# A hybrid decoder block on eight cores: the convolution's rows copied on chip, and the second tile's norm moved ahead

## The reference

```
x = x + 0.5 * swiglu(rmsnorm(x, ffn1_norm), ...)           # first feed-forward
h = rmsnorm(x, mix_norm); proj = h @ w_in                  # 1024 -> 6656
glu_a, glu_b, q, k, v, g_conv, g_attn = split(proj)
u = glu_a * sigmoid(glu_b)
u = causal_depthwise_conv(u, dw_w) + dw_b                  # width 31, along the tokens
conv_out = silu(layernorm(u)) @ w_proj
attn_out = sliding_window_gqa_sinks(rope(q), rope(k), v) @ w_o
x = x + (sigmoid(g_conv) * conv_out + sigmoid(g_attn) * attn_out) @ w_out
x = x + 0.5 * swiglu(rmsnorm(x, ffn2_norm), ...)           # second feed-forward
out = rmsnorm(x, final_norm)
```

## Time and profile before

| | us |
|---|---|
| three runs | 1957.9, 1786.0, 1765.6 (median 1786.0) |
| profiled execution | 1768.8 |
| its span on the slowest core (core 5) | 1767.8 |
| spans of the eight cores | 1748.8 to 1767.8 |
| PE busy | 1638.3 (93%) |

### The profile page before, as it was taken

How to read it: one execution, slowest core, us unless ns; L and a number is a source line. 1 busy time by engine, 2 the same in 40 slices (tenths; PEclk the granted TensorE clock), 3 DMA queues, 4 the chain that set the end, 5 groups by cost and what they waited for, 6 DMA issues and landing times.

```text
span 1767.8 us, 29593 instructions; the slowest of 8 cores (1748.8 to 1767.8 us)
## 1 busy us (share of the span) xinstructions
PE 1638.3 (93%) x9060; PEld 739.0 (42%) x9060; DVE 704.0 (40%) x1180; ACT 651.8 (37%) x1396; POOL 687.7 (39%) x723
## 2 busy tenths in 40 slices
PE   6999677899988899989999999999998999998996
PEld 2555333344433334434443344444443444443442
DVE  3432422764243365441225266542224356524212
ACT  3212312664132366443222257553222258422221
POOL 1014023865332595413331387423322277413232
PEclk9999788999999999999999999999999999999998
DMA  8998987579999999985556978764443953443542
GB/s 171 197 217 167 208 204 178 140 190 183 203 196 239 233 180 172 192 274 156 163 147 176 238 198 190 194 240 152 142 138 115 237 199 98 145 152 128 182 123 81
DMA packets 118121, 315.39 MB, mean 178 GB/s; under 512 B 14544, under 2 KB 36304, under 8 KB 117968
## 3 DMA queue, kind: packets, MB, share of 16 engines
q1 hardware_dynamic: 92480, 231.46, 41.8%
q0 software_dynamic: 24768, 80.95, 29.0%
q10 hardware_dynamic: 720, 1.09, 0.2%
HBM read 327.01 MB, written 67.37 MB: 223 GB/s over the span
## 4 chain that ended last, share of the span: by engine, by line
PE 80%; DMA 11%; issue 2%; ACT 2%; DVE 2%; SPq 2%; POOL 1%; ACTq 0%; DVEq 0%; POOLq 0%
PE ps L508 74%; PE ps L82 5%; DMA RR<-ush 3%; DMA ush<-S 3%; DMA ush<-uT 2%; SPq L98 2%; DMA X<-xT 1%; DMA wt<-wall 1%; PE ps L706 1%; DMA outT<-tf 1%; ACT ps L82 0%; POOL acc L82 0%; DVE xnF L82 0%; DVE S L82 0%; ACT S L82 0%
## 5 line engine op out<-in xcount | busy, mean ns | idle before, releaser
L508 PE MATMUL ps<-xnF,wt 128*128 128x512 bf16 x2816 | 652.1, 386 | 15.9 <-DVE xnF L82 6.5
L508 PEld LDWEIGHTS ps<-xnF,wt 128*128 128x128 bf16 x2816 | 270.0, 99 | 357.2 <-issue 64.3
L508 PE MATMUL ps<-Hh,wt 128*128 128x512 bf16 x1408 | 328.6, 380 | 0.0
L508 PE MATMUL ps<-xnM,wt 128*128 128x512 bf16 x1344 | 310.9, 383 | 0.4 <-DVE xnM L82 0.2
L82 ACT ACTIVATE tf<-ps 128x512 f32<-128x512 f32 x304 | 179.9, 595 | 312.5 <-PE ps L508 291.0
L82 POOL TENSOR_TENSOR Hh<-tf 128x512 bf16<-128x512 f32 x128 | 164.7, 1287 | 187.9 <-PE ps L508 115.1
L82 DVE SCALAR_TENSOR_TENSOR tf<-tf,ps 128x512 f32<-128x512 f32 x176 | 120.4, 684 | 260.8 <-PE ps L508 248.0
L508 PEld LDWEIGHTS ps<-Hh,wt 128*128 128x128 bf16 x1408 | 134.3, 98 | 160.8 <-issue 9.3
L508 PEld LDWEIGHTS ps<-xnM,wt 128*128 128x128 bf16 x1344 | 129.9, 98 | 169.7 <-issue 22.2
L98 POOL DMA_DIRECT2D wt<-wall x121 | 67.7, 563 | 245.6 <-PE ps L508 214.5
L82 DVE SCALAR_TENSOR_TENSOR X<-ps,X 128x512 f32<-128x512 f32 x96 | 66.3, 691 | 199.5 <-PE ps L508 197.5
(11 more groups left out here) (97 smaller groups left out, 1471.8 us busy)
## 6 DMA issues: line engine op xcount, KB each, us to landing
wt<-wac SPq DMA_DIRECT2D x207, 512.0 KB, 4.8
wt<-wall POOLq DMA_DIRECT2D x121, 512.0 KB, 9.7
wac<-wt SPq DMA_DIRECT2D x82, 512.0 KB, 8.7
wt<-wdc SPq DMA_DIRECT2D x80, 352.0 KB, 3.1
RR<-ush SPq DMA_DIRECT2D x128, 135.0 KB, 6.3
wt<-wd POOLq DMA_DIRECT2D x48, 352.0 KB, 7.1
wdc<-wt SPq DMA_DIRECT2D x32, 352.0 KB, 5.8
X<-xT SPq DMA_DIRECT2D x28, 256.0 KB, 10.8
```

The costliest lines, as they stand in the source:

```text
L508: op(PE, lambda: mm(out, lhsT=pick(use.slot), rhs=rhs, start=start, stop=stop), rd, wr, t, use)
```

## The change

- `ush` is gone. `uT` gets 32 more columns: column 31 on holds the tile's 512, columns 0 to 30 the 31 tokens ahead of it. For tile 0 these 31 are computed from the halo (31 columns in place of 128); for the others they are copied by DVE from `past`, where the tile before left them (two small copies a chunk).
- `u_in` copies from `uT` to `RR` within SBUF: 16 DMAs of 32 x 540 (one for each shift k and group g) in place of 4 of 32 x 4 x 540, all on SP.
- Tile 1's squares are summed on POOL into `accL` and its norm is written to `xnF` behind the first gate/up, that is during the first down projection. The load of `X[1]` has the same condition as before (`H_b[8]`).
- The halo's squares wait for tile 0's norm (`xnF_b[7]`).
- The planner's durations of a few small tasks are set by size, and a group of 8 or more DMAs is planned at 0.35 us each.

```diff
     def dma(self, q, dsem, moves, rd=(), wr=(), t=5.0):
...
-        k.t = 0.1 * len(moves)
+        k.t = (0.1 if len(moves) < 8 else 0.35) * len(moves)
...
-        uT = sb("uT", [128, 3, NT], BF16); uT_b = bufs(3)
+        uT = sb("uT", [128, 3, 32 + NT], BF16); uT_b = bufs(3)
+        past = sb("past", [128, 8, 32], BF16); past_b = bufs(8)
...
-            f_a_norm(t, banks.get())
+            if t != 1:
+                f_a_norm(t, banks.get())
             if t == 0:
                 bk = banks.get()
-                sums_pe(Xh, Xh_b, bk, HALO)
+                sums_pe(Xh, Xh_b, bk, HALO, (xnF_b[7],))
...
             ffn_gu(0, banks, t == 0)
             keep = G.key
+            if t == 0:
+                load_x(1, (H_b[8],))
+                for c in range(8):
+                    sq_acc(accL, c == 0, X[1][:, c, :], X_b[1][c], tm=tmM)
+                normed(rstd(accL, banks.get()), C_FFN1, X[1], X_b[1], xnF, xnF_b)
...
-            parts = [(xnM, xnM_b, NT, uT[:, cc % 3, :], uT_b[cc % 3], base, ush_s[cc % 3], ush_b[cc])]
+            u_t, u_b = uT[:, cc % 3, :], uT_b[cc % 3]
+            parts = [(xnM, xnM_b, 0, NT, u_t[:, 31:31 + NT])]
             if halo:
-                parts.append((xnh, xnh_b, HALO, uh[:, cc % 2, :], uh_b[cc % 2], 0, ushh_s[cc % 2], ushh_b[cc]))
+                parts.append((xnh, xnh_b, HALO - 31, 31, u_t[:, 0:31]))
+            else:
+                COPY(u_t[:, 0:31], past[:, cc, 0:31], (past_b[cc],), (u_b,), 0.15)
...
-                dma(SP, sem, [(ush_d[cc][:, c0:c0 + N], u_t)], rd=(u_b,), wr=(db,), t=6.0)
+            COPY(past[:, cc, 0:31], u_t[:, NT:NT + 31], (u_b,), (past_b[cc],), 0.15)
 
         def u_in(cc, base):
-            dma(SP, RR_s[cc % NRR], [(RR[cc % NRR][32 * k:32 * k + 32, :, :],
-                                      ush_d[cc][:, base - 31 + k:base - 31 + k + RW].rearrange("(g c) t -> c g t", g=4)) for k in range(4)],
-                rd=(ush_b[cc], ushh_b[cc]), wr=(RR_b[cc % NRR],), t=8.0)
+            dma(SP, RR_s[cc % NRR], [(RR[cc % NRR][32 * k:32 * k + 32, g, :], uT[32 * g:32 * g + 32, cc % 3, k:k + RW])
+                                     for k in range(4) for g in range(4)], rd=(uT_b[cc % 3],), wr=(RR_b[cc % NRR],), t=6.0)
```

More of the change, by code:

```diff
@@ L363, in build_nc @@
     wdc_d = dt("wdc", [32, 128, 11 * 128], BF16, kind="Internal").ap()
-    ush_d = dt("ush", [8, 128, TL], BF16, kind="Internal").ap()
     with ExitStack() as es:
@@ L399, in build_nc @@
         RR_s = [mksem(f"s_rr{i}") for i in range(NRR)]
-        ush_b = bufs(8); ush_s = [mksem(f"s_ush{i}") for i in range(3)]
         NW = 9
@@ L435, in build_nc @@
         s_pos = [mksem(f"s_pos{i}") for i in range(2)]
-        ushh_b = bufs(8); ushh_s = [mksem(f"s_ushh{i}") for i in range(2)]
-        uh = S[:].rearrange("p a b -> p (a b)")[:, 768:896].bitcast(BF16).rearrange("p (a b) -> p a b", a=2); uh_b = bufs(2)
         s_out = [mksem(f"s_out{i}") for i in range(8)]
@@ L480, in build_nc @@
         alias(cvo_b, Xh_b + Hhh_b + [accH[1]])
-        alias(S_b, xnh_b + uh_b + [cosh_b, sinh_b])
+        alias(S_b, xnh_b + [cosh_b, sinh_b])
         def ACTF(out, in_, func, rd, wr, t=None, **kw):
@@ L514, in load_x, with proj @@
                     rd=after, wr=(X_b[t % 2][c],), t=7.0)
-        def proj(pst, pb, use, sub, rhs_t, rhs_bufs, N):
+        def proj(pst, pb, use, sub, rhs_t, rhs_bufs, N, c0=0):
             G.join(True)
             for kc in range(8):
-                MMW(pst[:, 0:N], use, lambda s, kc=kc: s[:, kc, sub * 128:(sub + 1) * 128], rhs_t[:, kc, 0:N], kc == 0, kc == 7,
+                MMW(pst[:, 0:N], use, lambda s, kc=kc: s[:, kc, sub * 128:(sub + 1) * 128], rhs_t[:, kc, c0:c0 + N], kc == 0, kc == 7,
                     rhs_bufs[kc] if isinstance(rhs_bufs[kc], list) else [rhs_bufs[kc]], (pb,), t=N / 2360)
@@ L543, in rstd, with sums_pe @@
             return pst, pb
-        def sums_pe(x_t, x_bufs, bank, N):
+        def sums_pe(x_t, x_bufs, bank, N, after=()):
             pst, pb = bank
@@ L548, in sums_pe @@
                 s_t, s_b = sqF.get()
-                ACTF(s_t[:, 0:N], x_t[:, c, 0:N], AF.Square, (x_bufs[c],), (s_b,))
-                MM(pst[:, 0:N], ones[:], s_t[:, 0:N], c == 0, c == 7, (ones_b, s_b), (pb,))
+                ACTF(s_t[:, 0:N], x_t[:, c, 0:N], AF.Square, (x_bufs[c],) + after, (s_b,), t=0.2 + 0.42 * N / NT)
+                MM(pst[:, 0:N], ones[:], s_t[:, 0:N], c == 0, c == 7, (ones_b, s_b), (pb,), t=N / 2360)
         def normed(inv, gcol, x_t, x_bufs, out_t, out_bufs, N=NT):
@@ L725, in glu @@
             use = SA.use(("A", 28 + cc), "M")
-            parts = [(xnM, xnM_b, NT, uT[:, cc % 3, :], uT_b[cc % 3], base, ush_s[cc % 3], ush_b[cc])]
+            u_t, u_b = uT[:, cc % 3, :], uT_b[cc % 3]
+            parts = [(xnM, xnM_b, 0, NT, u_t[:, 31:31 + NT])]
             if halo:
-                parts.append((xnh, xnh_b, HALO, uh[:, cc % 2, :], uh_b[cc % 2], 0, ushh_s[cc % 2], ushh_b[cc]))
-            for xn_t, xn_bufs, N, u_t, u_b, c0, sem, db in parts:
+                parts.append((xnh, xnh_b, HALO - 31, 31, u_t[:, 0:31]))
+            else:
+                COPY(u_t[:, 0:31], past[:, cc, 0:31], (past_b[cc],), (u_b,), 0.15)
+            for xn_t, xn_bufs, c0, N, dst in parts:
                 pa, pab = bM5.get()
                 pb_, pbb = bM5.get()
-                proj(pb_, pbb, use, 1, xn_t, xn_bufs, N)
+                proj(pb_, pbb, use, 1, xn_t, xn_bufs, N, c0)
                 t_t, t_b = tmM.get()
-                ACTF(t_t[:, 0:N], pb_[:, 0:N], AF.Tanh, (pbb,), (t_b,), scale=0.5)
-                proj(pa, pab, use, 0, xn_t, xn_bufs, N)
-                STT(u_t, t_t[:, 0:N], 1.0, pa[:, 0:N], ALU.add, ALU.mult, (t_b, pab), (u_b,))
-                dma(SP, sem, [(ush_d[cc][:, c0:c0 + N], u_t)], rd=(u_b,), wr=(db,), t=6.0)
+                ACTF(t_t[:, 0:N], pb_[:, 0:N], AF.Tanh, (pbb,), (t_b,), t=0.2 + 0.4 * N / 512, scale=0.5)
+                proj(pa, pab, use, 0, xn_t, xn_bufs, N, c0)
+                STT(dst, t_t[:, 0:N], 1.0, pa[:, 0:N], ALU.add, ALU.mult, (t_b, pab), (u_b,), t=0.15 + 0.55 * N / 512)
+            COPY(past[:, cc, 0:31], u_t[:, NT:NT + 31], (u_b,), (past_b[cc],), 0.15)
         def u_in(cc, base):
-            dma(SP, RR_s[cc % NRR], [(RR[cc % NRR][32 * k:32 * k + 32, :, :],
-                                      ush_d[cc][:, base - 31 + k:base - 31 + k + RW].rearrange("(g c) t -> c g t", g=4)) for k in range(4)],
-                rd=(ush_b[cc], ushh_b[cc]), wr=(RR_b[cc % NRR],), t=8.0)
+            dma(SP, RR_s[cc % NRR], [(RR[cc % NRR][32 * k:32 * k + 32, g, :], uT[32 * g:32 * g + 32, cc % 3, k:k + RW])
+                                     for k in range(4) for g in range(4)], rd=(uT_b[cc % 3],), wr=(RR_b[cc % NRR],), t=6.0)
         taps = [None]
@@ L942, in build_nc @@
         load_pos(HALO, NT, cos_t, cos_b, (H_b[4],))
-        load_x(1, (H_b[8],))
         cdma(POOL, "ident", ident[:], ident_d, ident_b, (H_b[11],))
```

## The result

The change makes the kernel slower: a median of 1909.0 us (1872.2 to 2115.0, five runs) against 1772.6 (1765.6 to 1957.9, five runs), a ratio of **1.0569, 95% interval 1.0494 to 1.0644**. The highest times on both sides come from executions in which one die or both ran at a lower clock; the ratio leaves them out, and so isn't that of the two medians. The profiled execution took 1874.9 us, 106 more than the profiled one of before. The forecast was 1747, its range ended at 1790.

The account below looks back on a forecast made before the run. PE was taken as nearly full except in the convolution stages, mostly tile 0's, where SP's waits held it up. Gains of 23 + 8 - 4 - 7 + 2 = 22 us from 1768.8 gave 1747 us, range 1706 to 1790.

Parts of the forecast that it names:

- the price of an issue: SP's row copies: 0.40 us per DMA issue, 16 making 6.4 and, with another issue, 6.9 us a chunk.
- the break-even: All convolution stages: the change becomes a loss from 7.6 us of SP a chunk, an issue of 0.44.
- the bound of 0.99 under load: SP's row copies: upper bound on one issue, from eight issues under load that took 7.92 us.
- the rival at 0.60 an issue: SP as new bound, slower than before: 10.1 us a chunk, 1849 us; chance 0.19, half near 1782, half beyond 1804.
- tile 0 with the junction: Tile 0's convolution stage: gain 14.4 us, with the junction's 12.5 less 3.6 making 23.
- The junction: Behind the first down projection: 56 gate/up matmuls of tile 1 fill PE's half-idle 17 us, gain 12.5.
- DVE's wait: DVE's copy into uT, waiting for rows to leave the buffer: counted as nothing at 6.9 us a chunk.
- The weights in tile 0: Tile 0's convolution stage: SP's waits for weights were taken to stay at 24.0 us.
- Cheap issues: Rival: issues at 0.35 us and under, PE sets the pace, 1714 us (1700 to 1733); chance 0.27.
- Weight stream binds: Rival in tile 0: stage cannot become shorter than about 100 us, gain 14 becomes 5, 1756 us; chance 0.13.
- No overlap: Rival: small transfers don't overlap, 38 us a chunk, kernel over 2500 us; chance 0.01.
- The rule on small transfers: Row copies of 34.6 KB: many transfers under 64 KB should be coalesced, so the change would go the wrong way.

## Why the prediction was wrong

**The step that failed** is the price of an issue: "I take 0.40, between the unloaded rows and nearer to them than to the loaded one. 16 x 0.40 = 6.4, and one or so other issue per chunk [...] makes 6.9 us of SP per chunk". It measured 0.591 for the issue, 0.63 to 0.76 from start to start, and 11.9, 12.0, 11.7 and 11.4 us a chunk in tiles 0 to 3. The mechanism was as forecast: SP paces the convolutions. The size of this term was off, and with it the sign of the whole, since the break-even that the prediction named lay at 7.6 us a chunk.

The price was read from reads of device memory, the only RR rows that the trace had, and corrected downwards for fewer pieces. Both moves were wrong: between 32 and 128 pieces there is no difference (0.422 against 0.429 us from device memory, 0.591 against 0.588 from SBUF), while having the source in SBUF as well as the destination, which wasn't considered, adds 0.16 to 0.17 us. The prediction did name the bound of 0.99 under load and priced the rival at 0.60 an issue, 10.1 us a chunk, with 1849 us. That rival is what happened, with a chance of 0.19, half of it beyond 1804. Its 1849 is near the measured 1875, but partly because errors cancel. Its price per us of chunk, (1849 - 1782) / (10.1 - 8.0) = 32, carried to the 11.7 us that a chunk took on the mean makes 1849 + 51 = 1900. Against that stand landings of 2.4 us in place of 6 in four stages (14 less) and the 24.0 us of weight waits that it kept in tile 0 and that weren't there; the first u of tile 0, on the other hand, came 8.6 us later than it had it (see below). That gives about 1871, an estimate from these rows. The planner's wrong duration, worth about 1.5%, stood in no term of the sum.

By its terms, forecast and measured: tile 0 with the junction +23, in fact -10.2 at the last convolution; tile 1 +8, in fact -26.9; tile 2 -4, in fact -34.2; tile 3 -7, in fact -36.4.

**The junction** was right: full, at a clock of 1.00. Alone the move brings about 15 us (ratio 0.9918) where 12.5 less 3.6 stood in the sum. One step beside it was missed: 12.5 us of matmuls in 7.9 us of idle time also push the first u back, so "u of chunk 0 is there at 190.2" became 198.8 (197.80, plus 0.98 for its two parts). In the change the gain couldn't come out in tile 0, where SP set the end of the stage; it came back behind it, as the 9.4 us of the ledger.

**DVE's wait**: "so I count nothing; at 10 us a chunk it would be late". It was, for 170.7 us, and the condition was the right one. A fourth buffer took 29 us of it away and changed no time.

**The weights in tile 0**: the waits for them were taken as fixed at 24.0 us. In the profile after, SP's waits from 186 to 310 us hold none for `wt<-wall`: its issues fill the time in which it used to wait. So tile 0's stage, which was 100 us long already, grew by 1.9 us from its first u and not by 27 to 36, as the others did. "SP's waits for weights stay at 24.0" was a second step that failed, in the change's favour.

**The rivals.** Cheap issues: refuted by 0.591. Weight stream binds ("the stage cannot become shorter than about 100"): in the kernel with four on-chip DMAs the last convolution of tile 0 starts at 252.26, 55 us after the first u at 197.11; refuted. No overlap: refuted, 2.4 us landings behind issues of 0.6. **The rule on small transfers**, quoted in the prediction from the Trainium skill, "DMA: Bandwidth & Descriptors", "Rules for kernel authors", pointed the right way. What was paid by each, though, was SP's issue and not the transfer, which landed faster than the large ones (2.4 us against 6.3).

## What to carry to other kernels

Before a change multiplies the number of DMAs, count the issuing queue's time for one unit of work and set it against the time of the engine it feeds; and take the price of an issue from a row whose source and destination lie where yours do. When such a queue is full, share the work with an idle engine until neither is late, since moving all of it only moves the bound: 8 DMAs and 8 DVE copies a chunk gave 0.977, where 16 and 0 gave 1.057 (1.042 with the issues planned at what they take) and 0 and 16 gave 1.010. A wait at a buffer is tested by adding a buffer before it is called a cause.

## What the runs showed of the hardware

- An issue on SP from SBUF to SBUF took a median of 0.575 to 0.59 us, one from device memory to the same tile in SBUF 0.42 to 0.43; the shortest were 0.51 and 0.30. The medians were the same for 32 x 540 and 32 x 4 x 540. From SBUF to device memory it was 0.32 (weights, 128 x 2048) and 0.37 (u, 128 x 512). Why a copy with both ends in SBUF costs more, no run shows.
- Issues on SP and on ACT at the same time took 577 and 599 ns: there the two queues did not slow each other.
- A DVE copy of 32 x 540 bf16 from one block of 32 partitions to another took 0.29 us.
- A transfer of 34.6 KB (34,560 bytes) within SBUF landed in a median of 2.4 us when issued one by one every 0.6 us; four of four times the size, issued close together, in 6.7.
